# Router and decode blocks in 512-column halves, fp32r gate products, another order of index and last expert

## The reference

```
h = rmsnorm(x); q = h @ wq                       # 8 heads, two halves of 128 each: the router
s1, s2 = q halves @ keys1, keys2                 # 128 scores each; top 16 of each, top 16 of the 256 sums
gate = softmax(top 16 sums)                      # 8 heads x 16 = 128 picked experts of a token
act = gelu(h . u[expert]) * gate                 # decode: u is 16384 x 2048
x += sum over picks of act * v[expert]           # v is 16384 x 2048
out = rmsnorm(x)
```

## Time and profile before

| | |
|---|---|
| median of 3 runs | 2832.45 us (2830.51 to 2834.54) |
| profiled execution, its own time | 2833.08 us |
| its span, first to last instruction | 2831.2 us |
| PE busy | 2763.3 us (98%) |
| DVE, ACT, POOL busy | 1814.0, 1388.5, 251.2 us |
| granted TensorE clock, mean | 0.990 |
| router and decode, gates, late, experts | 280, 242.4, 356.6, 698.6 us |

### The profile page before, as it was taken

The page is one execution under the profiler, slowest core; times in us unless marked ns, Lnnn a source line. Parts: engine busy times, 40 slices in busy tenths (PEclk is TensorE's granted clock), DMA queues, the critical chain, the costliest instruction groups (busy, mean ns, idle before and its releaser), DMA issues.

```text
span 2831.2 us, 49456 instructions
## 1 busy us (share of the span) xinstructions
PE 2763.3 (98%) x15452; PEld 2414.6 (85%) x15452; DVE 1814.0 (64%) x2892; ACT 1388.5 (49%) x2016; POOL 251.2 (9%) x340
## 2 busy tenths in 40 slices
PE   8999999899999999999999999999999999999998
PEld 6888877788888888889999999888888888888886
DVE  6666655657986666578886666666664555555555
ACT  5454545545665444455555554555544444444444
POOL 0000000000000000000004997000000000000000
PEclk9999999999999999999999999999999999999999
DMA  6544454554554444555565454666665555555555
GB/s 245 188 148 167 159 178 150 169 202 144 172 166 164 156 156 141 181 196 184 185 207 174 159 160 153 219 210 214 210 205 179 193 193 193 192 193 193 193 192 191
DMA packets 153406, 514.70 MB, mean 182 GB/s; under 512 B 17040, under 2 KB 33680, under 8 KB 152208
## 3 DMA queue, kind: packets, MB, share of 16 engines
q1 hardware_dynamic: 131904, 482.54, 51.5%
q10 hardware_dynamic: 21456, 31.60, 3.1%
HBM read 501.49 MB, written 12.58 MB: 182 GB/s over the span
## 4 chain that ended last, share of the span: by engine, by line
PE 59%; DVE 1%; ACT 0%; issue 0%; DVEq 0%; POOL 0%; ACTq 0%; POOLq 0%
PE bank L482 12%; PE bank L2013 8%; PE bank L2014 8%; PE bank L2015 8%; PE bank L487 6%; PE bank L467 3%; PE bank L468 3%; PE bank L469 3%; PE bank L1988 2%; PE bank L522 1%; PE bank L521 1%; PE bank L520 1%; PE bank L1963 0%; DVE act L1027 0%; DVE big L1682 0%
## 5 line engine op out<-in xcount | busy, mean ns | idle before, releaser
L444 DVE TENSOR_TENSOR w_lo<-raw,w_hi 128x1024 fp32r<-128x1024 f32 x904 | 1098.3, 1225 | 827.5 <-ACT w_hi L435 822.7
L435 ACT ACTIVATE w_hi<-raw 128x1024 fp32r<-128x1024 f32 x904 | 953.5, 1059 | 1045.6 <-PE bank L2015 384.3
L482 PE MATMUL bank<-act,w_hi 128*128 128x512 f32 x3072 | 787.7, 398 | 4.5 <-ACT big L797 1.8
L482 PEld LDWEIGHTS bank<-act,w_hi 128*128 128x128 f32 x3072 | 554.4, 189 | 110.9 <-issue 5.5
L487 PEld LDWEIGHTS bank<-act,w_lo 128*128 128x128 f32 x3072 | 418.8, 190 | 31.1
L487 PE MATMUL bank<-act,w_lo 128*128 128x256 f32 x3072 | 427.8, 282 | 0.0
L2013 PE MATMUL bank<-w_hi,act 128*128 128x512 f32 x1024 | 399.5, 390 | 4.9 <-DVE act L1653 4.9
L2014 PE MATMUL bank<-w_lo,act 128*128 128x512 f32 x1024 | 399.1, 390 | 0.0
L2015 PE MATMUL bank<-w_hi,act 128*128 128x512 f32 x1024 | 399.1, 390 | 0.0
L467 PE MATMUL bank<-act,w_hi 128*128 128x256 f32 x912 | 261.6, 287 | 2.3 <-DVE w_lo L444 1.9
L469 PE MATMUL bank<-act,w_lo 128*128 128x256 f32 x912 | 259.4, 284 | 0.0
(11 more groups left out here) (276 smaller groups left out, 2344.8 us busy)
## 6 DMA issues: line engine op xcount, KB each, us to landing
raw<-in_stream SPq DMA_DIRECT2D x904, 512.0 KB, 3.3
big<-in_ukv ACTq DMA_DIRECT2D x16, 512.0 KB, 5.2
z_kept<-cst ACTq DMA_DIRECT2D x64, 128.0 KB, 3.2
cst<-z_kept ACTq DMA_DIRECT2D x64, 128.0 KB, 3.7
big<-in_x SPq DMA_DIRECT2D x2, 1024.0 KB, 9.5
big<-in_rows ACTq DMA_DIRECT2D x2, 1024.0 KB, 5.9
big<-in_rg_w ACTq DMA_DIRECT2D x1, 2048.0 KB, 8.1
x_kept<-big ACTq DMA_DIRECT2D x1, 2048.0 KB, 6.6
```

What stands on the lines that cost most here:

```text
L435: act.activation(w_hi[:, s, :], raw[:, s, :], ACT.Copy).then_inc(hi_ready, 1)
L444: dve.tensor_tensor(w_lo[:, s, :], raw[:, s, :], w_hi[:, s, :].bitcast(F32), ALU.subtract).then_inc(lo_ready, 1)
L482: pe.matmul(bank[:, :], w_hi[:, s, kk * P:(kk + 1) * P], act2[:, k, :, :].rearrange("p a n -> p (a n)"), start=(k == 0), stop=False)
```

## The change

Router and decode pairs go through `halves_out`. ACT copies the whole bank of 512 columns to SBUF (`copied`), POOL adds the two halves (`pool_summed`), and only then does ACT apply Gelu to the sum, or PE use the query. The gates stage gets 64 pairs with 4 tokens each instead of 32 with 8, and the late stage 32 instead of 64; 96 blocks are saved to DRAM instead of 64, of which 64 come back during the experts. The gate is split into high and low; DVE writes two fp32r tiles for a token instead of one, POOL one, and PE multiplies twice in fp32r. All four tokens' products stand behind the second unit. The expert operands get a tile of their own (it lies where `weighted` lay), so the first two are split before the last late turn. The index keys are turned first, the key-weight turn stands after the first query unit, and the first recurrent pair stands between the last two scores. The last two experts go token half by token half and bank by bank; the saved rows are loaded early into `big`; the end works bank by bank on DVE, ACT and POOL.

```diff
-         ("wqu", 4 * PH), ("u_decode", 2 * PH), ("u_gates", S // 8), ("u_late", NB // 2), ("v", NB)]
-EARLY = NB // 2
+         ("wqu", 4 * PH), ("u_decode", 2 * PH), ("u_gates", S // 4), ("u_late", NB // 4), ("v", NB)]
+EARLY = 3 * NB // 4
+LATE = NB - EARLY
...
+            def add_copied(dest, halves, block):
+                pool.wait_ge(copied, block + 5)
+                pool.tensor_tensor(dest, halves[:, 0:S], halves[:, S:2 * S], ALU.add).then_inc(pool_summed, 1)
...
+            def copy_halves(dest, bank, pair, block, before):
                 act.wait_ge(unit_done, 2 * pair + 2)
+                act.wait_ge(pool_summed, block + (5 - before))
+                act.activation(dest, bank[:, :], ACT.Copy).then_inc(copied, 1)
+            def early(pair, b2, n, block, before):
+                copy_halves(Z_HALVES[:, n, :], banks[2 + n], pair, block, before)
                 act.wait_ge(z_saved[n], b2 * 16 + 1)
-                act.activation(GZ[:, n, :], banks[2 + n][:, 0:S], ACT.Gelu).then_inc(gelu_ready[n], 1)
+                act.wait_ge(pool_summed, block + 5)
+                act.activation(GZ[:, n, :], Z_HALVES[:, n, 0:S], ACT.Gelu).then_inc(gelu_ready[n], 1)
...
-            with dve.Fori(0, S // 16) as i:
+            with dve.Fori(0, S // 8) as i:
                 for n in range(2):
-                    for s in range(8):
-                        ...
-                        if s % 4 == 3:
-                            ahead(split_lo, dve, "u_gates", i, 2, n, units=(s // 4,))
+                    for s in range(4):
+                        tok = i * 8 + (4 * n + s)
+                        dve.wait_ge(hot_used[s], i * 2 + n + 1)
+                        for part, weight in enumerate([gate_hi, gate_lo]):
+                            dve.tensor_scalar(weighted[:, s, part, :], iota, slot_t[:, 0, bass.ds(tok, 1)],
+                                              weight[:, bass.ds(tok, 1)], ALU.is_equal, ALU.mult).then_inc(hot1, 1)
+                        if s % 2:
+                            ahead(split_lo, dve, "u_gates", i, 2, n, units=(s // 2,))
                     add_halves(dve, GZ[:, n, :], banks[2 + n], block_of("u_gates", i, 2, n))
...
+                    halves_out(pe, pair_of("u_gates", i, 2, n), n, banks[2 + n])
+                    pe.wait_ge(gate_kept[n], i + 1)
+                    for s in range(4):
+                        pe.wait_ge(hot1, i * 16 + (8 * n + 2 * s + 2))
+                        pe.wait_ge(hot2, i * 8 + (4 * n + s + 1) + 1)
+                        pe.matmul(out_ap, hot[:, s, :], weighted[:, s, 0, :], start=True, stop=False)
+                        pe.matmul(out_ap, hot[:, s, :], weighted[:, s, 1, :], start=False, stop=True)\
+                          .then_inc(hot_used[s], 1)
...
+            index_scores(IH // 4 - 1, 0)
+            rnn_inputs(0)
+            index_scores(IH // 4 - 1, 1)
+            rnn_queries(0)
...
+            for u in range(2):
+                for n in range(2):
+                    pe.wait_ge(el_ready, NB - 1 + n)
+                    pe.wait_ge(lo_ready, UNITS - 3 + 2 * n + u)
+                    for cc in range(2):
+                        last_experts(0, u, n, cc)
+            for u in range(2):
+                for cc in range(2):
+                    for n in range(2):
+                        last_experts(1, u, n, cc)
```

More of the change, by code:

```diff
@@ L395, in build @@
         head_mixed = sem("head_mixed")
-        pq_kept = [sem(f"pq_kept{n}") for n in range(2)]
+        copied = sem("copied")
+        pool_summed = sem("pool_summed")
         ps_made = [sem(f"ps_made{n}") for n in range(2)]
@@ L813, in _ @@
                     index_queries(i, n + 2)
-            for n in range(2):
-                index_relu(IH // 4 - 1, n)
+            index_relu(IH // 4 - 1, 0)
+            ahead(split_hi, act, "rnn", 0, 2, 0, units=(0,))
+            index_relu(IH // 4 - 1, 1)
             act.wait_ge(softplus_ready, 3)
@@ L833, in rnn_block @@
             def rnn_block(j, first=False):
-                ahead(split_hi, act, "rnn", j, 2, 0, units=(0,))
+                if not first:
+                    ahead(split_hi, act, "rnn", j, 2, 0, units=(0,))
                 act.wait_ge(unit_done, 2 * pair_of("rnn", j, 2, 0) + 2)
@@ new lines, in _ @@
+            with act.Fori((EARLY - LATE) // 2, NB // 2 - 8) as i:
+                next_experts(i)
+            act.wait_ge(el_ready, FINAL_FREE)
+            act.wait_ge(x_saved, 16)
+            act.dma_start(XF, x_kept.rearrange("p (t n) -> p t n", t=TT)).then_inc(xf_ready, 16)
+            act.dma_start(final_row, rows[2, :, :]).then_inc(final_ready, 16)
+            with act.Fori(NB // 2 - 8, NB // 2 - 2) as i:
+                next_experts(i)
+            last = NB // 2 - 2
+            ahead(split_hi, act, "v", last, 2, 0)
@@ L1015, in _ @@
+            act.wait_ge(gained, 1)
+            act.wait_ge(fin_rstd, 1)
+            final_scale(0, slice(0, 1024))
+            final_squares(1, 2)
+            final_squares(1, 3)
+            final_root(1)
+            act.wait_ge(gained, 2)
+            act.wait_ge(fin_rstd, 2)
+            for q in range(2):
+                final_scale(1, slice(q * 512, (q + 1) * 512))
         @block.vector
@@ L1676, in _ @@
[L1676 to L1684 removed]
+                dve.wait_ge(act_ready[n], LATE // 2 + 1)
@@ new lines, in _, with add_expert_bank @@
+            with dve.Fori((EARLY - LATE) // 2, NB // 2 - 2) as i:
+                for n in range(2):
+                    next_expert(i, n)
+            last = NB // 2 - 2
+            ahead(split_lo, dve, "v", last, 2, 0)
+            expert_lo(last * 2 + 2, 0, last * 2 + 3)
+            ahead(split_lo, dve, "v", last, 2, 1, units=(0,))
+            expert_lo(last * 2 + 3, 1, last * 2 + 4)
+            ahead(split_lo, dve, "v", last, 2, 1, units=(1,))
+            def add_expert_bank(t, cb):
+                dve.wait_ge(bank_done, 4 * t + cb + 1)
+                xs = XF[:, t, cb * 512:(cb + 1) * 512]
+                dve.tensor_tensor(xs, xs, banks[4 * t + cb][:, :], ALU.add).then_inc(y_added, 1)
```

345 lines of the change are left out of this document (212 added, 133 removed).

## The result

The changed kernel took 2849.9 us (2848.6 to 2851.3), the one before 2832.5 (2830.5 to 2834.5): 1.0059 of the time before, 95% interval 1.0043 to 1.0075, some 17 us slower. The forecast was 2828, its range ended at 2846. The profiled execution took 2849.5 us, its span 2847.6.

The account below looks back on a forecast made before the run. PE's streaming, and helpers so late that PE stops, were taken to bound the kernel. Terms -6 + 20 + 0 - 6.5 - 6.8 - 5.3 = -4.6 from 2833.1, less 0.6, gave 2828 us; range 2808 to 2846.

Parts of the forecast that it names:

- Router: Router pairs in halves: 8 heads save 6.0 us of PE streaming, of which 5 was taken.
- first expert: Start of the experts: a tile of its own lets the split finish before, -6.8 us (-7 to -2).
- end: From last product to span's end: 12.8 us falls to 7.5, -5.3 us (-7 to -2).
- saved blocks: 32 more blocks through DRAM, their products in VectorE's idle time during the experts: 0, at most 40 us if uncovered.
- Index: Index stage: keys turned first, a recurrent pair between the last scores, less creeping after stops: -6.5 us (-8 to 0).
- Gates and late: Gates and late stages: token 3's tiles come late, PE waits, 6.87 us a pair: +20 us (-8 to +52).
- Decode: Decode pairs in halves: 16 pairs save 3.0 us, of which 1 was taken, the rest lost to scores after an add.
- Rival D: Router and decode: the round trip saturates ScalarE; decode +8 for -1, router 3 more: 2840; chance 0.12.
- B: Gates: tiles for tokens 2 and 3 are ready in time, so -8 and not +20: 2800; chance 0.18.
- C: Gates: narrow 128-column products are as dear as 512 columns (0.227 us), +52 for the stage: 2860; chance 0.12.
- E: Gates bound by ScalarE's order between two splits: 7.0 us or more a pair, 2836 and up; counted to A's upper side.
- A: The forecast itself: 2818 to 2838 us, chance 0.52; about a third of it below 2826.8, counted as faster.

Follow-up runs that it names:

- tiles first: Changed kernel with VectorE writing all four tokens' tiles of the next gates pair ahead of the low split: 2810.3 us, 0.9917 of the kernel before.
- fp32: Changed kernel with one tile and one fp32 product for each gates token, gate not split: 2825.5 us, 0.9975 of the kernel before.

## Why the prediction was wrong

1. **Router, first expert, end, saved blocks, experts' VectorE load**: right by mechanism and size (table above). **Index**: the size was luck in part. The recurrent pair between the scores gave its share, but turning the keys first gave 0.5 of its 1.9, and 1.45 came from the clock behind that stop, which the sum had counted behind the later stops and not behind this one.
2. **Gates and late, the step that failed in size: "I take 6.87 for the pair"**. The mechanism was the forecast's own, and it is shown from both sides: more time ahead of the tiles' deadline (tiles first) or fewer tiles (fp32) removes the stop. The term was mis-sized in three places, in sum 15.8 us. Late and gates pairs run at 5.59 and 6.93, not 5.57 and 6.87: some 4. Every second pair bears 0.28 more, 9 us; there the loop's jump stands bare, 0.18 of idle time, since PE has just been held. Taking half of the jumps away gave back 2.2 where 4.5 would be their share, with a later split of ScalarE in the third pair; so half of the 9 is shown to go with PE's jump, and the rest stays open. And the first pair cost 10.5, 3.6 over its share, where 1 was taken: its tiles come only after ScalarE's copies of the picks, and behind the wait for the picks the granted clock was 0.65 in its first 3 us. The jump is what the trace before could not show directly: there PE never waited at the end of a turn, so its jumps were free. That a restart costs more than its weight loads should have made the bound wider upwards.
3. **Decode, "1 of the 3.0": wrong by 4.7 us, by mechanism.** Rival D described it, with the add at 0.9 or more, and in the second decode loop it came at 1.47 and more; the router, where D expected 3 us, lost nothing. The working had counted one table load for a pair, from the earlier trace rows, and hidden it beside the add; it is two for two pairs, one of them at the loop's head, beside nothing. It had also halved and doubled a mean of 841 ns that hid two groups, 0.60 without a split beside it and 1.47 with one. And no term asked what is late when PE comes 4.6 us earlier after the first score: the picks were ready less than 2 us ahead of PE before. The first expert had been read with that question, what is late next; decode had not.
4. **Rivals.** B (no stop in the gates, 2800) was the state that one reordering brings: 2810. C is refuted at 0.110 a product. E's number, 7.0 or more a pair, came true without its cause: ScalarE's order stops nothing once the tiles stand first. D's 2840 holds the forecast's gates term, and E's 2836 its decode term; E's and D's terms together give some 2848, near what came; that was priced nowhere and lies above the range.
5. **The working itself.** Two slips moved nothing: the estimate of 41 us for the 512 products lies 23 under the tokens' 64, not 20; and a third of A's 0.52 is 0.17, where 0.22 went into the chance of faster.

## What to carry to other kernels

When a change makes a helper's work twice as long behind an instruction that waits, move the work ahead of the wait before asking for its price: here the order of ten instructions decided between +17 and -22 us. When several engines hand work round, a stop taken away alone is mostly found again one step on; list what is ready how long before it is wanted, and mend the stops together. And a loop whose engine waits at its end pays for its jump; where nothing waited, no idle time stood at the loop's end. A mean of durations is worth splitting before it is scaled: two groups can stand behind it.

## What the hardware showed

- A 128-column fp32r product with its own weights costs 0.110 us, hardly less than one of 256 columns (0.12): halving the columns gives next to nothing, and each product more costs its full 0.110.
- PE's jump back at a loop's end costs some 0.2 to 0.3 us when PE has just been held, and nothing that can be seen otherwise (32 waits of 0.18 in the changed kernel, 15 with half the turns, none with the tiles first).
- ScalarE's second decode loop, entered behind an exponential and repeated behind a Gelu, loads a table at its head in each turn, 1.28 us behind 1.06 of idle time, even ahead of a plain copy; behind a dummy Gelu its turns have no load.
- A 128x256 add on GpSimd takes 0.73 us beside VectorE's searches, and 1.29 to 2.6 when 0.68 us or more of a VectorE split lies beside it.
- Behind stops of PE of 1.3 to 4.9 us the granted clock was 0.50 to 0.77 over the next 3 to 7 us, and eight 512-column products took 3.56 us instead of 2.14; but behind the stops of 1.51 in the index stage and 1.12 in decode it stayed at 1.00.
